# High and low parts of weighted expert rows stacked on the two halves of the partitions

## The chip, the cores and the metric

The kernel runs on one core of a Trainium2 chip. The metric is the device time of one launch in microseconds (us). All matrices of the kernel are float32; TensorE (PE) takes them either as float32 or as fp32r, the 32-bit format in which one product takes one pass over the columns.

## The reference

One decoder block over 512 tokens of width 1024. After two attention branches, whose code the change does not touch, a router picks 4 of 32 experts for each token, and the result is

```
gate    = softmax(top-4 logits)
gu      = xb @ w_gate_up[e] + b_gate_up[e]        # xb: rows of the tokens that chose expert e
a       = (clip(u) + 1) * (min(g) * sigmoid(1.702 * min(g)))
yb      = a @ w_down[e] + b_down[e]
y       = segment_sum(yb * gate, token of the row)
out     = x + y
```

## The kernel before

The first 450 us or so are norm, projections, attention and routing. Then comes the expert stage, which the change touches. It works through items. An item is one expert's list of up to 96 tokens (even items, three groups of 32 rows) or up to 64 tokens (odd items, two groups). There are 32 items here: item 0, then a hardware loop (`Fori`) of 15 pairs, each with an odd item (i = 1) and an even item (i = 2), and a last odd item outside the loop.

For each item PE runs `gate_up(i)` (line 1712: 8 slices k of 128 input features, products of 32 stationary columns and 512 moving ones, four side by side on the array) and `down(i)` (line 1751, and line 1759 for the third group). In one turn of the loop PE's order is gate_up(1), the small list products (line 1658), down(0), gate_up(2), lists, down(1). The weights are float32, 2 MB for each DMA: four for gate_up (`gu_head` three, `gu_tail` one) and two for down (`dn_even` or `dn_odd`), issued by SP in a fixed order. Each has one buffer, and SP issues the next transfer into it when PE has read it (`gu_used`, `bank_done`, `dn_used`).

`down` leaves the rows of an item in PSUM: bank 5 holds slots 0 to 63 on partitions 0 to 63 with columns 0 to 511 of the model width, and the same slots on partitions 64 to 127 with columns 512 to 1023. Bank 4 holds the third group of an even item, in the same two halves. They are weighted by the tokens' gates and split in two fp32r tiles: ScalarE (ACT) writes the high part `y_hi` (`weigh`, line 849), and when all of an item's are written (`y_high`) VectorE (DVE) writes the rest `y_lo` (`keep_low`, line 1245) and signals `y_kept`. An even item has two such tiles (n = 0, 1), an odd one has one (n = 2).

The sum over experts for each token is made on PE by one-hot tables: `put_odd`, `put_even` and `put_even_b`, made by POOL, have a 1 where slot (partition) belongs to token (column); partitions 64 to 127 repeat the slots of 0 to 63. For each 128 tokens (a chunk c, of four) `sums` (line 1678) multiplies the chunk's columns of a table with `y_hi` and `y_lo`. Partitions 0 to 63 go into the bank of columns 0 to 511 and partitions 64 to 127 into the bank of 512 to 1023. `add_sums` on DVE (line 1253) adds both banks to the residual `x_tok`.

The order around it is written out by hand. The four chunks of a pair of items (the even item of this turn's down(0) and the odd item of the turn before) stand inside gate_up(2), after the slices k = 1, 3, 5 and 6 (`SUM_STEPS`). Chunk 0 waits for `y_kept` of the pair (line 1686). The semaphore `gu_used` of slice k = 1 is raised ahead of that wait. After the loop, `gate_up(1, last=True)` holds down(0) after k = 3, chunk 0 after k = 5 and chunk 1 after k = 6; chunks 2 and 3, down(1) and the four last sums (the last item alone, one table) follow, and SP stores each chunk of `x_tok` as it is complete. In all there are 64 full chunks and 4 last ones. On DVE, `keep_low(i - 1)` is the last step of a turn's half, behind `activate(i)`; on ACT, `weigh(i - 1)` stands behind `sigmoid(i)`.

Of the kernel before, what the change touches and what calls it, by code (L numbers as in the profile page):

```python
# [20 lines left out]
F32 = mybir.dt.float32  # L21
F32R = mybir.dt.float32r
BF16 = mybir.dt.bfloat16
I32 = mybir.dt.int32
ALU = mybir.AluOpType
ACT = mybir.ActivationFunctionType
AX = mybir.AxisListType

P = 128
HD = 64  # L30
# [26 lines left out]
def hybrid_block(nc, x, positions, norm1_g, w_in, b_forget, b_gate, q_norm_swa, k_norm_swa, sinks,  # L57
                 q_norm_fox, k_norm_fox, w_o_swa, w_o_fox, w_out, norm2_g, w_router, b_router,
                 w_gate_up, b_gate_up, w_down, b_down, out):
    T, D = x.shape[1:]  # L60
# [38 lines left out]
    with ExitStack() as ctx:  # L99
# [30 lines left out]
        xreg, r1, r2, work, const = Region(16 * K), Region(32 * K), Region(36 * K), Region(10 * K), Region(17 * K)  # L130
# [50 lines left out]
        xT = r2.put("xT", [P, KD, SLOTS])  # L181
        aT = r2.put("aT", [P, KD, SLOTS])
        y_at = r2.at
        y_hi = [r2.put(f"y_hi{n}", [P, D // 2], F32R) for n in range(3)]
        y_lo = [r2.put(f"y_lo{n}", [P, D // 2], F32R) for n in range(3)]
        y_end = r2.at
        sel = r2.put("sel", [P, NB, 2, P], BF16)

# [83 lines left out]
        put_odd = in_place_of("w_rt", "put_odd", [P, T], F32R)  # L272
# [52 lines left out]
        gate_all = r1.put("gate_all", [P, ITEMS, 2])  # L325

        ps = ctx.enter_context(nc.psum_tensor("ps", [P, 8, 512], F32))
# [75 lines left out]
        y_high, y_kept, put_ready = sem("y_high"), sem("y_kept"), sem("put_ready")  # L403
# [155 lines left out]
        def _(pool):  # L559
            steps = [0]  # L560

            def then(ins):

                steps[0] += 1
                ins.then_inc(pool_step, 1)
                pool.wait_ge(pool_step, steps[0])

            g = nc.gpsimd
# [43 lines left out]
            for i in range(E):  # L612
                ins = g.memset(place_rank[:, i:i + 1], float(E - 1 if i == 0 else i // 2 if i % 2 else N_SMALL + i // 2 - 1))
# [37 lines left out]
            pool.wait_ge(items_ready, 1)  # L651
            n_pairs = pool.value_load(pairs[0:1, 0:1], min_val=PAIRS, max_val=MAX_PAIRS)
            pool.wait_ge(bdn_ps, 8)
            g.memset(y_hi[2][:, :].bitcast(F32), 0.0)
            then(g.memset(y_lo[2][:, :].bitcast(F32), 0.0))
            g.tensor_copy(put_odd[:, :], y_lo[2][:, :].bitcast(F32)).then_inc(put_ready, 1)
            then(g.tensor_copy(put_row[:, 1:3], row_all[:, 0, :]))
            put(put_even, 1)
            put(put_even_b, 2)
# [24 lines left out]
        def _(act):  # L684
            sc = nc.scalar
# [24 lines left out]
            for k in range(KD):  # L710
                act.wait_ge(hT_ps, k + 1)
                sc.activation(hT_h[:, k, :], ps[:, k % 4, :], ACT.Identity,
                              scale=vcol[:, k:k + 1]).then_inc(hT_hi, 1)
# [18 lines left out]
            for g in range(G_GATE, G_O):  # L732
                c = g - G_GATE
                split_high(g + 1)
                if g == G_O - 1:
# [3 lines left out]
                    for r in (0, 64):  # L739
                        ins = sc.activation(c_rows[r:r + 32, :], ps[r:r + 32, 7, :], ACT.Copy, scale=-1.0 / SCALE)  # L740
# [17 lines left out]
                for d in (0, 1):  # L758
                    j = 2 * c + d
                    ins = sc.activation(gates_T[:, j, :], ps[:, g % 2 * 2 + d, :], ACT.Sigmoid,  # L760
                                        bias=vcol[:, 16 + j:17 + j])
# [4 lines left out]
            for n in range(1, len(QKT), 2):  # L766
                s, j = QKT[n]
                act.wait_ge(qkT_ps, n + 1)
                dst, src, scale = turned(s, j)
# [10 lines left out]
            for n in range(NU):  # L780
# [3 lines left out]
                if n >= 4:  # L784
# [3 lines left out]
                              scale=SCALE, accum_out=den[:, n:n + 1]).then_inc(probs, 1)  # L788
# [24 lines left out]
            for m in range(N_OUT):  # L813
# [5 lines left out]
                for c in range(NB):  # L819
                    s = slice(m * GW, (m + 1) * GW)  # L820
                    ins = sc.activation(h2n[:, c, s], x_tok[:, c, s], ACT.Square, accum_out=ssq_g[:, m, c:c + 1])
# [22 lines left out]
            def weigh(i, pair=None):  # L844

                col = slice(i, i + 1) if pair is None else bass.ds(pair * 2 + i, 1)
                act.wait_ge(dn_used[1], counted(2, i + 1, pair))
                for a in (0,) if i % 2 else (0, 1):
                    ins = sc.activation(y_hi[i % 2 * 2 + a][:, :], ps[:, 5 - a, :], ACT.Identity,
                                        scale=gate_all[:, col, a:a + 1].rearrange("p a n -> p (a n)"))  # L850
                ins.then_inc(y_high, 1)

            sigmoid(0)
# [12 lines left out]
        def _(dve):  # L866
            v = nc.vector
# [24 lines left out]
            for k in range(KD):  # L892
                dve.wait_ge(hT_hi, k + 1)
                v.scalar_tensor_tensor(out=hT_l[:, k, :], in0=ps[:, k % 4, :], scalar=vcol[:, k:k + 1],
                                       in1=hT_h[:, k, :].bitcast(F32), op0=ALU.mult,
                                       op1=ALU.subtract).then_inc(hT_ready, 1)
# [11 lines left out]
            for n in range(3):  # L908
                ins = v.tensor_scalar(above[:, n:n + 1], row, float(GROUP * (n + 1)), None, ALU.is_ge)
# [4 lines left out]
                                        op0=ALU.mult, op1=ALU.add))  # L914
            then(v.tensor_scalar(place_of[:, 1:2], place_of[:, 1:2], float(SMALL), None, ALU.add))
            then(v.scalar_tensor_tensor(out=place_of[:, 0:1], in0=above[:, 1:2], scalar=-2.0 * GROUP, in1=row,
                                        op0=ALU.mult, op1=ALU.add))
# [12 lines left out]
            for part in (C1, C2, C3):  # L930
                then(v.scalar_tensor_tensor(out=ang[:, :, :], in0=ang_k[:, :, :], scalar=-part, in1=ang[:, :, :],
                                            op0=ALU.mult, op1=ALU.add))
            v.tensor_scalar(ang[:, :, :], ang[:, :, :], 3.1415925, -3.1415925, ALU.min, ALU.max).then_inc(ang_ready, 1)
            v.tensor_scalar(sink_neg[:, :], sink_bc[:, :], -1.0, None, ALU.mult)
            for g in range(2, G_GATE + 1):
                split_low(g)
                if g == G_GATE:
# [8 lines left out]
                                   op0=ALU.mult, op1=ALU.max).then_inc(fl_abs, 1)  # L946
# [4 lines left out]
            for g in range(G_GATE, G_O):  # L951
                c = g - G_GATE
# [7 lines left out]
                if c == 1:  # L960
# [5 lines left out]
                    for a in (0, 1):  # L966
# [5 lines left out]
                                                    in1=g2, op0=ALU.mult, op1=ALU.mult))  # L972
                if 2 <= c < NB + 2:
# [4 lines left out]
                    for a, h0, h1 in ((0, 0, HQ), (1, HQ, SWA_H)):  # L978
                        n = h1 - h0
# [6 lines left out]
                    for half in (0, 1):  # L986
                        ins = v.tensor_tensor(k_dup[:, c, :, half, :], rot[:, 0, HQ:SWA_H, :], rot[:, 1, HQ:SWA_H, :],
                                              ALU.add)
                    ins.then_inc(qk_ready, 1)
                if g == G_GATE + 5:  # L990

                    dve.wait_ge(fl_ln, 1)
                    for at in range(0, P, 32):
                        ins = v.scalar_tensor_tensor(out=lf[:, :, at:at + HF], in0=fl[:, :, :], scalar=0.0,
                                                     in1=fl_a[:, :, :], op0=ALU.min, op1=ALU.subtract)
# [3 lines left out]
            for r in (32, 96):  # L999
                ins = v.scalar_tensor_tensor(out=c_rows[r:r + 32, :], in0=ps[r:r + 32, 7, :], scalar=-1.0 / SCALE,  # L1000
                                             in1=c_hi[r:r + 32, :].bitcast(F32), op0=ALU.mult, op1=ALU.subtract)
            ins.then_inc(c_ready, 1)

            for n in range(0, len(QKT), 2):
                s, j = QKT[n]
                dve.wait_ge(qkT_ps, n + 1)
                dst, src, scale = turned(s, j)
# [16 lines left out]
            for p in range(NP + 3):  # L1024
                if p < NP:
                    n = 2 * p
                    c, b, h = units[n]
# [4 lines left out]
                    if b == 0:  # L1032
                        v.scalar_tensor_tensor(out=nb[:, two], in0=mx[:, two], scalar=-SCALE, in1=sink_neg[:, h:h + 2],
                                               op0=ALU.mult, op1=ALU.min).then_inc(shift, 1)
# [77 lines left out]
            for c in range(NB):  # L1112
                ins = v.scalar_tensor_tensor(out=lg[:, c, :], in0=ps[:, 7, c * E:(c + 1) * E], scalar=rstd[:, 1, c:c + 1],
                                             in1=brt[:, :], op0=ALU.mult, op1=ALU.add)
# [124 lines left out]
            def keep_low(i, pair=None):  # L1239

                col = slice(i, i + 1) if pair is None else bass.ds(pair * 2 + i, 1)
                dve.wait_ge(y_high, counted(2, i + 1, pair))
                for a in (0,) if i % 2 else (0, 1):
                    n = i % 2 * 2 + a
                    ins = v.scalar_tensor_tensor(out=y_lo[n][:, :], in0=ps[:, 5 - a, :],
                                                 scalar=gate_all[:, col, a:a + 1].rearrange("p a n -> p (a n)"),
                                                 in1=y_hi[n][:, :].bitcast(F32), op0=ALU.mult, op1=ALU.subtract)
                ins.then_inc(y_kept, 1)

            def add_sums(c, n, banks=SUM_BANKS):  # L1250
# [121 lines left out]
        def _(pe):  # L1372
# [298 lines left out]
            def sums(parts, c, n, banks=SUM_BANKS):  # L1671

                pe.wait_ge(sums_added, n)
                for at, (table, y) in enumerate(parts):
                    for half in (y_hi[y], y_lo[y]):
                        for h in (0, 1):
                            rows = slice(h * HD, (h + 1) * HD)
                            ins = pe.matmul(ps[:, banks, :][:, h], table[rows, c * P:(c + 1) * P], half[rows, :],  # L1678
                                            start=(at == 0 and half is y_hi[y]),
                                            stop=(at == len(parts) - 1 and half is y_lo[y]))  # L1680
                return ins

            def pair_sums(c, pair, banks=SUM_BANKS, added=None):
# [140 lines left out]
```

## Time and profile before

| | |
|---|---|
| median of 3 runs | 1443.29 us (1440.86 to 1443.79) |
| the profiled execution: its span, from first to last instruction | 1443.0 us |
| PE busy | 1375.7 us (95%) |
| DVE busy | 747.1 us (52%) |
| ACT busy | 220.7 us (15%) |
| moved by DMA | 447.27 MB, mean 310 GB/s |
| granted TensorE clock, mean | 0.989 |

For the profiled execution the page gives no time beside its span; the median of the runs lies 0.29 us above that span. Busy times overlap, so they do not add up to the span. A row of the timeline gives the start of a group of instructions, the time from the start of its first to the end of its last, and their number.

### The profile page before, as it was taken

The numbers are of one execution on the slowest core, as the hardware profiler recorded it, in microseconds if no ns is written. First come the engines' busy times: TensorE is split into PE (matmuls) and PEld (weight loads), VectorE is DVE, ScalarE is ACT, GpSimd is POOL, SyncE is SP. The second block draws the span as 40 slices with busy tenths as digits, with TensorE's granted clock in tenths as the row PEclk, the third lists the DMA queues.
The fourth block names the chain that finished last, engine by engine and source line by source line (L and its number), as shares of the span: only waits on it lengthen the run. The fifth ranks groups of instructions, "written<-read, shape, count | busy, mean of one in ns | idle before, by whom it ended". The sixth has DMA issues, their size and how long they took to land.

```text
span 1443.0 us, 27407 instructions
## 1 busy us (share of the span) xinstructions
PE 1375.7 (95%) x11224; PEld 660.7 (46%) x11227; DVE 747.1 (52%) x1472; ACT 220.7 (15%) x398; POOL 185.6 (13%) x234
## 2 busy tenths in 40 slices
PE   6999999999988999999999999999999999999997
PEld 5888887878952333333232323323232332323233
DVE  5213745666256565645556444555654455565444
ACT  4224435552220000000000000000000000000000
POOL 2001400000002021120211202021120202112020
PEclk9999999999999999999999999999999999999999
DMA  6232320002769999999999999999999999999992
GB/s 190 88 117 67 109 88 1 2 30 89 277 242 354 414 386 413 399 410 413 412 413 400 419 395 413 411 413 414 400 421 401 413 411 412 411 399 419 401 412 119
DMA packets 59127, 447.27 MB, mean 310 GB/s; under 512 B 8592, under 2 KB 26032, under 8 KB 34480
## 3 DMA queue, kind: packets, MB, share of 16 engines
q1 hardware_dynamic: 55904, 435.96, 75.5%
q0 software_dynamic: 3072, 10.49, 2.3%
q8 instruction: 27, 0.44, 0.1%
q10 hardware_dynamic: 112, 0.28, 0.1%
q14 instruction: 12, 0.10, 0.0%
HBM read 442.51 MB, written 4.19 MB: 310 GB/s over the span
## 4 chain that ended last, share of the span: by engine, by line
PE 76%; DMA 20%; DVE 2%; ACT 1%; issue 1%; SPq 0%; DVEq 0%; ACTq 0%
PE ps L1712 31%; DMA gu_head<-in_w_gate_up_dram 11%; PE ps L1751 10%; DMA gu_tail<-in_w_gate_up_dram 8%; PE ps L1678 6%; PE ps L1406 3%; PE ps L1408 3%; PE ps L1407 3%; PE ps L1759 2%; PE ps L1543 2%; PE ps L1432 2%; PE ps L1431 2%; PE ps L1430 2%; PE ps L1397 1%; PE ps L1398 1%; PE ps L1399 1%
## 5 line engine op out<-in xcount | busy, mean ns | idle before, releaser
L1712 PE MATMUL ps<-gu_head,xT 128*32 128x512 f32 x3840 | 428.0, 596 | 8.2 <-DVE xT L1209 4.9
L1712 PEld LDWEIGHTS ps<-gu_head,xT 128*32 128x32 f32 x3840 | 120.5, 110 | 292.0 <-issue 276.0
L1253 DVE TENSOR_TENSOR x_tok<-x_tok,ps 128x1024 f32<-128x1024 f32 x68 | 82.7, 1220 | 255.8 <-PE ps L1678 255.8
L1712 PE MATMUL ps<-gu_tail,xT 128*32 128x512 f32 x1280 | 157.3, 630 | 27.7 <-DMA gu_tail<-in_w_gate_up_dram 27.7
L842 ACT ACTIVATE act_s<-act_gu 128x768 f32<-128x768 f32 (+1 forms) x32 | 23.6, 738 | 935.6 <-DVE act_gu L1228 935.6
L1205 DVE STREAM_TRANSPOSE xT<-xg 32x256 f32<-32x256 f32 x308 | 132.9, 432 | 3.8
L1217 DVE STREAM_TRANSPOSE act_gu<-ps 128x512 f32<-128x512 f32 x80 | 57.2, 715 | 143.3 <-PE ps L1712 138.2
L638 POOL DMA_INDIRECT xg<-h_dram,idx_g x32 | 70.0, 2187 | 446.1 <-DVE row_all L1187 446.1
L1751 PE MATMUL ps<-dn_even,aT 128*32 128x512 f32 x1024 | 116.1, 594 | 0.0
L879 DVE TENSOR_TENSOR st_l<-st_w,st_h 128x2048 fp32r<-128x2048 f32 x25 | 57.3, 2292 | 113.2 <-ACT st_h L702 113.2
L1751 PE MATMUL ps<-dn_odd,aT 128*32 128x512 f32 x1024 | 113.2, 594 | 2.2 <-DVE aT L1236 2.2
L1712 PEld LDWEIGHTS ps<-gu_tail,xT 128*32 128x32 f32 x1280 | 38.6, 114 | 128.5 <-issue 89.9
L1751 PEld LDWEIGHTS ps<-dn_odd,aT 128*32 128x32 f32 x1024 | 31.6, 110 | 70.0 <-issue 67.0
L1751 PEld LDWEIGHTS ps<-dn_even,aT 128*32 128x32 f32 x1024 | 31.7, 110 | 68.0 <-issue 67.6
L1759 PE MATMUL ps<-dn_even,aT 128*32 128x512 f32 x512 | 60.8, 592 | 0.0
L702 ACT CAST st_h<-st_w 128x2048 fp32r<-128x2048 f32 x25 | 47.7, 1908 | 32.7 <-PE ps L1432 30.1
L666 POOL COPY put_row<-row_all 128x1 f32 x15 | 2.8, 186 | 383.9 <-PE ps L1678 383.9
L1406 PE MATMUL ps<-hT_h,st_h 128*128 128x512 f32 x128 | 50.0, 391 | 0.0
L1430 PE MATMUL ps<-st_h,hT_h 128*128 128x512 f32 x128 | 49.9, 390 | 0.0
L1408 PE MATMUL ps<-hT_h,st_l 128*128 128x512 f32 x128 | 49.8, 389 | 0.0
L1407 PE MATMUL ps<-hT_l,st_h 128*128 128x512 f32 x128 | 49.8, 389 | 0.0
L1432 PE MATMUL ps<-st_h,hT_l 128*128 128x512 f32 x128 | 49.8, 389 | 0.0
(361 smaller groups left out, 1814.4 us busy)
## 6 DMA issues: line engine op xcount, KB each, us to landing
gu_head<-in_w_gate_up_dram SPq DMA_DIRECT2D x96, 2048.0 KB
gu_tail<-in_w_gate_up_dram SPq DMA_DIRECT2D x32, 2048.0 KB, 20.3
dn_even<-in_w_down_dram SPq DMA_DIRECT2D x32, 2048.0 KB, 25.1
dn_odd<-in_w_down_dram SPq DMA_DIRECT2D x32, 2048.0 KB, 21.3
st_w<-in_w_in_dram SPq DMA_DIRECT2D x17, 1024.0 KB, 5.2
st_w<-in_w_out_dram SPq DMA_DIRECT2D x4, 1024.0 KB, 5.4
x_tok<-in_x_dram SPq DMA_DIRECT2D x4, 512.0 KB, 6.0
st_w<-in_w_o_swa_dram SPq DMA_DIRECT2D x4, 512.0 KB, 3.5
```

The costliest lines, as they stand in the source:

```text
L638: g.indirect_dma_start(out=xg[0:n, :], out_offset=None, in_=h2_dram[:, :], in_offset=bass.IndirectOffsetOnAxis(ap=idx_g[0:n, 0:1], axis=0) ...
L1205: ins = v.transpose(xT[r, :, s].rearrange("r (k a) s -> r k a s", a=2), near[s, r].rearrange("s p k a -> s k a p"))
L1253: v.tensor_tensor(x_tok[:, c, :].rearrange("p (h n) -> p h n", h=2), x_tok[:, c, :].rearrange("p (h n) -> p h n", h=2), ps[:, banks, :], A ...
L1406: pe.matmul(dst, wh[:, k], xh[:, k], start=(k == 0), stop=False)
L1407: pe.matmul(dst, wh[:, k], xl[:, k], start=False, stop=False)
L1408: ins = pe.matmul(dst, wl[:, k], xh[:, k], start=False, stop=(k == n - 1))
L1430: pe.matmul(dst, hT_h[:, k0 + k, rows], st_h_wide[half][:, k], start=(half == 0 and k == 0), stop=False)
L1432: ins = pe.matmul(dst, hT_l[:, k0 + k, rows], st_h_wide[half][:, k], start=False, stop=(half == 1 and k == KH - 1))
L1678: ins = pe.matmul(ps[:, banks, :][:, h], table[rows, c * P:(c + 1) * P], half[rows, :], start=(at == 0 and half is y_hi[y]), stop=(at == l ...
L1712: ins = pe.matmul(ps[j * GROUP:(j + 1) * GROUP, n, :], xT[:, k, n * GROUP:(n + 1) * GROUP], gu_columns(k, j), start=(k == 0), stop=(k == K ...
L1751: ins = pe.matmul(ps[u * GROUP:(u + 1) * GROUP, 5, :], aT[:, 4 * j + k, u % 2 * GROUP:(u % 2 + 1) * GROUP], dn_chunk(i, j)[:, k * D + u // ...
L1759: ins = pe.matmul(ps[u * GROUP:(u + 1) * GROUP, 4, :], aT[:, 4 * j + ku, 2 * GROUP:], dn_chunk(i, j)[:, ku * D + u // 2 * 512:ku * D + (u ...
```

## The change

Instead of a tile of high parts and one of low parts, each tile now holds one half of the model width (h = 0: columns 0 to 511, h = 1: columns 512 to 1023), with the high parts on the partitions that have this half in PSUM and the low parts on the other 64 partitions. ACT writes 64 partitions at a time, and DVE reads PSUM and the high part on one half of the partitions and writes on the other half. `sums` then contracts all 128 partitions in one product for each table and half of the width. The tiles take the same place. The lines that zero `y_half[2]` at the start are renamed only.

```diff
-        y_hi = [r2.put(f"y_hi{n}", [P, D // 2], F32R) for n in range(3)]
-        y_lo = [r2.put(f"y_lo{n}", [P, D // 2], F32R) for n in range(3)]
+        y_half = [[r2.put(f"y_half{n}{h}", [P, D // 2], F32R) for h in (0, 1)] for n in range(3)]
...
                 for a in (0,) if i % 2 else (0, 1):
-                    ins = sc.activation(y_hi[i % 2 * 2 + a][:, :], ps[:, 5 - a, :], ACT.Identity,
-                                        scale=gate_all[:, col, a:a + 1].rearrange("p a n -> p (a n)"))
+                    for h in (0, 1):
+                        high = slice(h * HD, (h + 1) * HD)
+                        ins = sc.activation(y_half[i % 2 * 2 + a][h][high, :], ps[high, 5 - a, :], ACT.Identity,
+                                            scale=gate_all[high, col, a:a + 1].rearrange("p a n -> p (a n)"))
                 ins.then_inc(y_high, 1)
...
                 for a in (0,) if i % 2 else (0, 1):
-                    n = i % 2 * 2 + a
-                    ins = v.scalar_tensor_tensor(out=y_lo[n][:, :], in0=ps[:, 5 - a, :],
-                                                 scalar=gate_all[:, col, a:a + 1].rearrange("p a n -> p (a n)"),
-                                                 in1=y_hi[n][:, :].bitcast(F32), op0=ALU.mult, op1=ALU.subtract)
+                    for h in (0, 1):
+                        high, low = slice(h * HD, (h + 1) * HD), slice((1 - h) * HD, (2 - h) * HD)
+                        y = y_half[i % 2 * 2 + a][h]
+                        ins = v.scalar_tensor_tensor(out=y[low, :], in0=ps[high, 5 - a, :],
+                                                     scalar=gate_all[high, col, a:a + 1].rearrange("p a n -> p (a n)"),
+                                                     in1=y[high, :].bitcast(F32), op0=ALU.mult, op1=ALU.subtract)
                 ins.then_inc(y_kept, 1)
...
                 for at, (table, y) in enumerate(parts):
-                    for half in (y_hi[y], y_lo[y]):
-                        for h in (0, 1):
-                            rows = slice(h * HD, (h + 1) * HD)
-                            ins = pe.matmul(ps[:, banks, :][:, h], table[rows, c * P:(c + 1) * P], half[rows, :],
-                                            start=(at == 0 and half is y_hi[y]),
-                                            stop=(at == len(parts) - 1 and half is y_lo[y]))
+                    for h in (0, 1):
+                        ins = pe.matmul(ps[:, banks, :][:, h], table[:, c * P:(c + 1) * P], y_half[y][h][:, :],
+                                        start=(at == 0), stop=(at == len(parts) - 1))
```

## Rows read from the trace of the kernel before

**Rows 1.** The page's slices of 36 us: DMA share in tenths, and GB/s.
```profile
DMA  6232320002769999999999999999999999999992
GB/s 190 88 117 67 109 88 1 2 30 89 277 242 354 414 386 413 399 410 413 412 413 400 419 395 413 411 413 414 400 421 401 413 411 412 411 399 419 401 412 119
```
**Rows 2.** Busy time by stretch: us, busy of each engine, clock, DMA share, GB/s.
```profile
510.00:515.00 5.00, 5.00 (x56) 1.59 (x52) 4.73 (x11) 0.00 (x0) 3.71 (x3) 1.00 0.72 239
...
860.00:920.00 60.00, 57.47 (x528) 18.20 (x520) 33.31 (x67) 3.32 (x5) 9.49 (x7) 1.00 1.01 411
```
**Rows 3.** PE's waits on weights, timeline: start, us, instructions, [idle before, releaser].
```profile
900.29 3.64 PE L1712 MATMUL ps<-gu_tail,xT 128*32 128x512 f32 x32 [2.10 <-DMA gu_tail<-in_w_gate_up_dram]
...
914.98 5.36 PE L1712 MATMUL ps<-gu_head,xT 128*32 128x512 f32 x48 [0.43 <-DMA gu_head<-in_w_gate_up_dram]
...
1341.48 5.34 PE L1712 MATMUL ps<-gu_tail,xT 128*32 128x512 f32 x32 [2.92 <-DMA gu_tail<-in_w_gate_up_dram]
```
**Rows 4.** The chain of waits, around one chunk of sums and the list products.
```profile
842.44 0.19 PE ps L1658 x4
...
865.10 1.59 PE ps L1678 x12
```
**Rows 5.** PE's timeline, a run of products of 128 rows by 512 columns, first and last.
```profile
59.71 0.39 PE L1431 MATMUL ps<-st_l,hT_h 128*128 128x512 f32 x1
...
65.15 0.39 PE L1431 MATMUL ps<-st_l,hT_h 128*128 128x512 f32 x1
```
**Rows 6.** PE's timeline, inside one chunk of sums.
```profile
920.27 0.50 PE L1678 MATMUL ps<-y_hi,put_odd 64*128 64x512 f32 x2
920.61 0.39 PE L1678 MATMUL ps<-y_lo,put_odd 64*128 64x512 f32 x2
...
921.53 0.40 PE L1678 MATMUL ps<-y_lo,put_even_b 64*128 64x512 f32 x2
```
**Rows 7.** Groups of ACT and DVE: busy us, mean ns | idle before; then single lines.
```profile
L849 ACT ACTIVATE y_hi<-ps,gate_all 128x512 fp32r<-128x512 f32 x48 | 31.0, 680 | 25.6 <-PE ps L1759 14.6 <-PE ps L1751 9.1
...
L1245 DVE SCALAR_TENSOR_TENSOR y_lo<-ps,gate_all,y_hi 128x512 fp32r<-128x512 f32 x48 | 34.5, 746 | 21.1 <-ACT y_hi L849 19.8
...
L740 ACT ACTIVATE c_rows<-ps x2: 572/582/592, 205.3 to 205.9; 32x512 fp32r<-32x512 f32 x2
...
207.31 1.39 DVE L1000 SCALAR_TENSOR_TENSOR c_rows<-ps,c_hi 32x512 fp32r<-32x512 f32 x2
```
**Rows 8.** Timeline of the last turn of the loop: ACT, DVE and PE.
```profile
1357.61 1.26 ACT L849 ACTIVATE y_hi<-ps,gate_all 128x512 fp32r<-128x512 f32 x2
...
1359.03 1.41 DVE L1245 SCALAR_TENSOR_TENSOR y_lo<-ps,gate_all,y_hi 128x512 fp32r<-128x512 f32 x2
...
1362.53 0.50 PE L1678 MATMUL ps<-y_hi,put_odd 64*128 64x512 f32 x2
```
**Rows 9.** Timeline after the loop, down to the final sums.
```profile
1409.59 1.26 ACT L849 ACTIVATE y_hi<-ps,gate_all 128x512 fp32r<-128x512 f32 x2 [14.57 <-PE ps L1759]
...
1411.00 1.41 DVE L1245 SCALAR_TENSOR_TENSOR y_lo<-ps,gate_all,y_hi 128x512 fp32r<-128x512 f32 x2 [13.90 <-ACT y_hi L849]
...
1412.79 0.50 PE L1678 MATMUL ps<-y_hi,put_odd 64*128 64x512 f32 x2
...
1424.92 7.07 PE L1751 MATMUL ps<-dn_odd,aT 128*32 128x512 f32 x64 [2.18 <-DVE aT L1236]
...
1433.00 0.75 DVE L1245 SCALAR_TENSOR_TENSOR y_lo<-ps,gate_all,y_hi 128x512 fp32r<-128x512 f32 x1 [5.87 <-ACT y_hi L849]
1433.97 0.50 PE L1678 MATMUL ps<-y_hi,put_odd 64*128 64x512 f32 x2 [1.97 <-DVE y_lo L1245]
...
1434.60 0.64 PE L1678 MATMUL ps<-y_hi,put_odd 64*128 64x512 f32 x2
1434.85 4.61 DVE L1253 TENSOR_TENSOR x_tok<-x_tok,ps 128x1024 f32<-128x1024 f32 x4 [1.10 <-PE ps L1678]
1435.02 0.64 PE L1678 MATMUL ps<-y_lo,put_odd 64*128 64x512 f32 x2
```

More of the change, by code:

```diff
@@ L653, in _ @@
             pool.wait_ge(bdn_ps, 8)
-            g.memset(y_hi[2][:, :].bitcast(F32), 0.0)
-            then(g.memset(y_lo[2][:, :].bitcast(F32), 0.0))
-            g.tensor_copy(put_odd[:, :], y_lo[2][:, :].bitcast(F32)).then_inc(put_ready, 1)
+            g.memset(y_half[2][0][:, :].bitcast(F32), 0.0)
+            then(g.memset(y_half[2][1][:, :].bitcast(F32), 0.0))
+            g.tensor_copy(put_odd[:, :], y_half[2][1][:, :].bitcast(F32)).then_inc(put_ready, 1)
             then(g.tensor_copy(put_row[:, 1:3], row_all[:, 0, :]))
```

## The prediction

> **What bounds the kernel now.** I read the page's 40 slices first. From slice 14 on, where the expert stage runs, DMA is at nine tenths or more and moves about 410 GB/s [rows 1], while PE is also nearly always busy, so the two have to be told apart. The stretches do that: 860 to 920 us has a DMA share of 1.01 with PE busy 57.5 of 60 us [rows 2]. The timeline of PE then shows where PE's 2 to 3 idle us go: it waits for weights, 2.10 us at 900, 0.43 at 915, 2.92 at 1341 [rows 3], a pattern that repeats from 648 us on (20 waits, small ones included). So in the middle of the loop the bound is the stream of weights, and PE has a little slack in each turn, about 2.5 to 3 us in 60.
>
> At both ends it is otherwise. The last wait of PE on weights is at 1341.48 [rows 3]. From there PE runs without a break up to 1422.7, and then the chain goes over DVE and ACT, with waits of 2.18 and 1.97 us [rows 9]. What delays PE after 1341 delays the end. At the start, DMA's share falls to 0.72 at 510 to 515 us [rows 2]: the transfers in flight had run out, and the next one waits for the end of gate_up(2) on PE. What delays PE before that moment delays the stream, which then bounds all that follows.
>
> **The products.** A full chunk has 12 products of 64 rows now. They start two by two, the two halves of the rows at once: the second pair at 920.61 and the sixth at 921.53, that is 0.92 us for four steps, 0.23 us a step, and 0.34 us for the first [rows 6]. A product of 128 rows by 512 columns takes (65.15 - 59.71) / 24 = 0.227 us in a dense run [rows 5], 24 products apart. So six pairs become six full products of the same length. The chunk costs PE 1.59 us now [rows 4], of which 6 x 0.227 = 1.36 is the products and 0.23 the change from the 32-column tiles of gate_up and back. Afterwards the latter is at least 0 and at most what it is now, or 0.1 more if a load of the whole array has to wait for all four tiles. The nearest row is the group of four list products, full-array as well: 0.19 us with that change in it [rows 4]. Five columns a product cost little, so about 0.16 for the change. I take a chunk as 1.52, 0.07 less than now; bounds -0.23 and +0.1. Half as many products, and next to nothing gained, since the halves already ran side by side.
>
> Of the 64 full chunks only those on a PE-bound piece count: four before 511 us, four in the last turn, two after the loop, ten in all. That gives -0.7 us (bounds -2.3 and +1.0). The other 54 lie beside the DMA stream.
>
> **ACT and DVE.** Instructions double: 48 to 96 on each. The length goes by the columns, not the partitions, by the nearest rows: 32x512 out of PSUM takes ACT 0.58 us against 0.68 for 128x512 with a scale, and the two DVE operations on 32 partitions take 1.39 together, against 1.41 for two of 128 [rows 7, 8]. On ACT two in a row take 1.26, a pitch of 0.58; four take 3 x 0.58 + 0.68 = 2.42 or a bit over, 2.45, so +1.19 for an even item and +0.59 for an odd one.
>
> On DVE two in a row take 1.41 with 0.746 each [rows 7, 8], so they overlap by 0.08. The two of line 1000, which lie on partitions 32 and 96, take 1.39 at 0.69 each: no overlap [rows 7]. The new ones alternate between the halves of the partitions, as those do. So four take 4 x 0.75 = 3.0 (bounds: 2.75 with the overlap; 3.2 if crossing the halves costs a further 0.05 each), +1.6 for an even item, and two take 1.5, +0.75 for an odd one. The page "VectorE: DVE Perf Modes" of the Trainium skill, section "Two Vector instructions with no wait between them", has a rule for this: an instruction that starts in another quadrant of partitions than the one before is held until all earlier ones have finished. By that rule it is 3.0, without it 2.75; the trace, with 1.39 against 1.41, agrees with it. Below zero these costs can't go, as nothing is taken off either engine.
>
> ACT is 15% busy and DVE 52%, so their throughput is not the matter. What counts is the chain: down's end, ACT, DVE, sums of chunk 0. Queued behind keep_low on DVE are the next list choice (1.6 us, needed some 20 us later) and add_sums of chunk 0, which moves back by less than the 5 us until PE asks for it. Behind weigh on ACT there is nothing for over 20 us.
>
> **The waits that this makes.** In a turn like the last one, y_hi starts at 1357.61 and PE starts chunk 0 at 1362.53 [rows 8]. After: ACT ends at 1357.61 + 2.45 = 1360.06; DVE starts 0.16 later as now, and ends at 1363.2; PE follows 0.22 later (from 1433.75 to 1433.97 now [rows 9]), at 1363.4: a new wait of **0.9 us**. In turns where PE has first waited for gu_head, as at 914.98, chunk 0 comes some 0.6 us later against ACT, and the wait is about 0.3. In the middle of the loop both are paid out of PE's idle time on weights: the queue of transfers is 20 us deep, and the buffer of slice 1 is handed back ahead of the wait. At two places they are not hidden:
> - the first turn, before the dry spell of DMA at 510: +0.9 (bound below 0, if the stream makes it up);
> - the last turn, after 1341: +0.9 (bound below 0.6, with DVE's overlap).
>
> **After the loop** down(0) ends only two slices of gate_up ahead of chunk 0. y_hi starts at 1409.59, y_lo ends at 1412.41 and PE starts at 1412.79 [rows 9]: 0.16 us of slack. After: 1409.59 + 2.45 + 0.16 + 3.0 + 0.22 = 1415.4, a new wait of **2.6 us** (2.3 with DVE's overlap) in PE's path. Behind it are the rest of gate_up(1), its turning by DVE and down(1), so it is paid in full.
>
> **At the very end** weigh(1) and keep_low(1) lie bare between down(1) and the last sums: 0.59 + 0.75 = **+1.34 us**. The last sums have two steps a chunk before and after, and DVE's four additions at 1.15 us each bound them [rows 9], so only the first chunk counts. PE's wait grows from 1.97 to 3.3 us. A wait of 2.92 was followed by the half clock (32 products in 5.34 us), 2.10 and 2.18 by the full one (32 in 3.64) [rows 3, 9]. So I take half clock for the first chunk: 0.42 and 0.64 (the rows at 1434.60 and 1435.02 [rows 9]), 1.1 us instead of 0.88: +0.25.
>
> **The clock after the new wait of 2.6.** A wait of 2.9 us costs 5.34 - 3.64, 1.7 us, by the lower clock of 1.2 GHz; one of 2.1 costs nothing [rows 3]. 2.55 lies midway between 2.18 and 2.92, so I can't name a nearer row, and take half the price, +0.85 (bounds 0 and 1.7).
>
> **The sum**, against the profiled execution: first turn 0.9, last turn 0.9, after the loop 2.6, end 1.34 + 0.25, clock 0.85, products -0.7. That is 6.1 us on 1443.0; the median is 0.3 above that span, and I keep that distance: 1443.3 + 6.1 = **1449.4**. With the terms at their small ends (0, 0.6, 2.3, 1.3, 0, -2.3 for the products) it is +1.9, 1445.2; with the large ones (0.9, 1.1, 2.8, 1.7, 1.7, +1.0) it is +9.2, 1452.5.
>
> **Rivals.**
> *The waits are paid in every turn.* If the DMA stream follows PE more closely than its share of 1.01 says, 14 more turns pay, half of them 0.9 and half 0.3, 8.4 us: 1457.8. For it: each weight tile has one buffer, so transfers start when PE lets go. Against it: in the middle of the loop PE waits for DMA and not the reverse [rows 2, 3]. 10%.
> *The new waits stay hidden*, since half the partitions are done in less time than the 32-partition rows say, and only the bare end is paid: 1.34 + 0.25 - 0.7 = +0.9, 1444.2. Both operations would have to take about half of now. Rows 7 speak against it. 10%.
> *The other side: a chunk of full products takes half of its time.* The halves then only seem to run side by side and the 12 products really cost 12 issues. A chunk would fall from 1.59 to 0.8; ten exposed ones give -8 against +6.8 of the other terms: 1442.1, not slower. It decides from 0.68 us saved a chunk on, and would be plain in PE's busy time. Against it: the dense step of 0.227 us [rows 5] can't be beaten by the same instruction. If the dry spell of DMA at 510 is spared as well, it comes to 1440. 5%.
> *The clock gives back.* If the later arrival shortens the wait at 1341 below about 2.2 us, 1.7 us return. Its turn has a new wait of only 0.3, less four chunks at -0.07, so the wait stays 2.9. 5%: 1447.7, within the range.
>
> **Numbers.** The forecast's case has 70%, with a range of its own of 1445.2 to 1452.5. A difference of 0.2%, 2.9 us, is about what a measurement can tell. Slower by over that holds for nearly all of the forecast's case, the clock's rival and the first rival: 0.79. Within it: the hidden case, most of the third rival, and the low end of the forecast: 0.17. Faster: 0.04. The range of 8 in 10 reaches down to the hidden case and leaves the rival at 1458 out: 1444.0 to 1453.5.
>
> **What would show it.** Right: 96 operations on each of lines 849 and 1245 at unchanged length; even items with a row of four of 2.45 us on ACT and 3.0 on DVE; chunks of six products at 1.4 to 1.6 us; a wait of PE on DVE before chunk 0, some 0.9 or 0.3 us in the loop and 2.6 after it; DMA share still 1.01 in the loop, and PE's waits on weights shorter by what the new ones take. Wrong: chunks clearly under 1.4 us; operations on 64 partitions shorter than 0.5 us; turns longer than 63 us in the middle of the loop.

## The result, and the profile after

| | before | after |
|---|---|---|
| median (lowest to highest) | 1442.47 us (1440.86 to 1443.79), 4 runs | 1451.88 us (1449.37 to 1453.5), 4 runs |
| ratio, 95% interval | | 1.006 (1.0038 to 1.0081) |
| span of the profiled execution | 1443.0 us | 1451.7 us (its run took 1453.5) |

The change makes the kernel 0.6% slower: 9.4 us between the medians, 8.7 between the profiled spans. The forecast was 1449.4, with 1444.0 to 1453.5 as range. A run's time lies about 1.8 us above its own span (1453.5 and 1451.7 here), so the profiled execution of before belongs to a run of about 1444.8 (an estimate from this distance). Both profiled executions are thus on the slow side of their kernels, by about the same amount.

The page of the changed kernel, part 5 (busy us, mean ns | idle before) and part 2 (DMA's busy tenths in slices, nine or more through the loop as before). The instructions of ACT and DVE are twice as many, at the length of before:

```profile
L1248 DVE SCALAR_TENSOR_TENSOR y_half<-ps,gate_all,y_half 64x512 fp32r<-64x512 f32 x96 | 72.0, 750 | 48.1 <-ACT y_half L850 46.7
...
L850 ACT ACTIVATE y_half<-ps,gate_all 64x512 fp32r<-64x512 f32 x96 | 65.6, 683 | 27.7 <-PE ps L1759 13.7
...
DMA  6232320003678999999999999999999999999981
```

DVE had 746 ns and ACT 680 at 128 partitions [rows 7]: 64 partitions cost as much as 128.

The chain of waits after, one chunk of sums in the last turn of the loop. It is six products of 128 rows in 1.59 us, where it was twelve of 64 rows in 1.59 [rows 4]:

```profile
1364.81 5.29 PE ps L1712 x48
1370.09 1.59 PE ps L1679 x6
```

PE's timeline after, with what it idled for ([idle before, releaser]): two turns in the middle of the loop, and then from the last wait on weights to the end. Against [rows 3, 8, 9]:

```profile
963.54 5.19 PE L1712 MATMUL ps<-gu_tail,xT 128*32 128x512 f32 x32 [2.41 <-DMA gu_tail<-in_w_gate_up_dram]
985.73 0.71 PE L1679 MATMUL ps<-y_half,put_odd 128*128 128x512 f32 x2 [1.23 <-DVE y_half L1248]
1026.25 3.64 PE L1712 MATMUL ps<-gu_tail,xT 128*32 128x512 f32 x32 [0.51 <-DMA gu_tail<-in_w_gate_up_dram]
1040.83 5.36 PE L1712 MATMUL ps<-gu_head,xT 128*32 128x512 f32 x48 [0.31 <-DMA gu_head<-in_w_gate_up_dram]
1046.89 0.71 PE L1679 MATMUL ps<-y_half,put_odd 128*128 128x512 f32 x2 [0.70 <-DVE y_half L1248]
1088.95 5.34 PE L1712 MATMUL ps<-gu_tail,xT 128*32 128x512 f32 x32 [2.04 <-DMA gu_tail<-in_w_gate_up_dram]
...
1340.84 5.34 PE L1712 MATMUL ps<-gu_tail,xT 128*32 128x512 f32 x32 [2.54 <-DMA gu_tail<-in_w_gate_up_dram]
1363.17 0.71 PE L1679 MATMUL ps<-y_half,put_odd 128*128 128x512 f32 x2 [1.22 <-DVE y_half L1248]
...
1416.42 0.70 PE L1679 MATMUL ps<-y_half,put_odd 128*128 128x512 f32 x2 [2.94 <-DVE y_half L1248]
...
1418.52 2.97 PE L1712 MATMUL ps<-gu_tail,xT 128*32 128x512 f32 x16
...
1430.11 8.77 PE L1751 MATMUL ps<-dn_odd,aT 128*32 128x512 f32 x64 [2.18 <-DVE aT L1237]
1442.31 3.77 PE L1679 MATMUL ps<-y_half,put_odd 128*128 128x512 f32 x8 [3.43 <-DVE y_half L1248]
```

The lines with "DVE y_half" as releaser are the new waits; only the one at the very end takes the place of an old one (1.97 us before [rows 9]). "Half clock" below means a stretch in which PE was granted the lower of its two clocks, 1.2 instead of 2.4 GHz: 32 products of gate_up behind a wait then take up to 5.34 us where they take 3.64 at the full one.

The two kernels have their last wait on weights within 0.7 us of each other (1341.48 and 1340.84), so the loop has lost nothing that one can see here. In these two traces all of the loss lies behind that point: 101.5 us remained before, 110.9 remain now. Piece by piece, from starts in this fence and in [rows 3, 8, 9]:

| piece | before | after | lost |
|---|---|---|---|
| last wait on weights to chunk 0 of the last turn | 21.05 | 22.33 | 1.3 |
| to chunk 0 after the loop | 50.26 | 53.25 | 3.0 |
| to the last down | 12.13 | 13.69 | 1.6 |
| to the last sums | 9.05 | 12.20 | 3.1 |
| to the end | 9.03 | 9.39 | 0.4 |

In the loop the waits on weights have shrunk: 0.51 + 0.31 + 2.04 from 1026 to 1089, where the same two turns had 1.72 + 0.42 + 2.85 before. The 2.1 us that are gone are about what the two new waits take, 1.93. Over the whole loop, the last wait on weights included, the waits on weights fell from 30.7 us (20 of them) to 18.8 (17), against 13.7 us in 14 new waits. Of those on `gu_tail`, five were followed by half clock after and six before, at 1.7 us each. So the agreement at 1341 holds some luck of the clock, and two single traces can't exclude a cost of a microsecond or so in the loop; e3 below has its bounds.

ACT's and DVE's timeline after, behind the last turn of the loop:

```profile
1410.21 2.77 ACT L850 ACTIVATE y_half<-ps,gate_all 64x512 fp32r<-64x512 f32 x4 [13.74 <-PE ps L1759]
1439.05 1.38 ACT L850 ACTIVATE y_half<-ps,gate_all 64x512 fp32r<-64x512 f32 x2 [10.81 <-PE ps L1751]
```
```profile
1413.13 3.04 DVE L1248 SCALAR_TENSOR_TENSOR y_half<-ps,gate_all,y_half 64x512 fp32r<-64x512 f32 x4 [14.53 <-ACT y_half L850]
...
1440.58 1.51 DVE L1248 SCALAR_TENSOR_TENSOR y_half<-ps,gate_all,y_half 64x512 fp32r<-64x512 f32 x2 [8.26 <-ACT y_half L850]
```

### The profile page after: what moved, and what is told of

Read it like the earlier page. It is cut to its first block, busy times and chain, and to the rows that moved or that the text cites. A ratio compares the mean times of both kernels' runs of the same rounds, so it can differ in the third digit from the quotient of the medians.

```text
span 1451.7 us, 26818 instructions
## 1 busy us (share of the span) xinstructions
PE 1377.7 (95%) x10835; PEld 662.1 (46%) x10835; DVE 784.6 (54%) x1520; ACT 256.8 (18%) x446; POOL 185.6 (13%) x234
## 4 chain that ended last, share of the span: by engine, by line
PE 63%; DMA 15%; DVE 12%; issue 4%; ACT 4%; DVEq 2%; ACTq 0%; SPq 0%; POOL 0%
PE ps L1712 26%; DMA gu_tail<-in_w_gate_up_dram 14%; PE ps L1679 7%; DVE xT L1206 6%; PE ps L1409 3%; PE ps L1751 3%; PE ps L1411 3%; PE ps L1410 3%; ACT y_half L850 2%; PE ps L1546 2%; PE ps L1435 2%; PE ps L1434 2%; PE ps L1433 2%; DVE y_half L1248 2%; DVE act_gu L1227 1%
## 5 line engine op out<-in xcount | busy, mean ns | idle before, releaser
L1248 DVE SCALAR_TENSOR_TENSOR y_half<-ps,gate_all,y_half 64x512 fp32r<-64x512 f32 x96 | 72.0, 750 | 48.1 <-ACT y_half L850 46.7
L850 ACT ACTIVATE y_half<-ps,gate_all 64x512 fp32r<-64x512 f32 x96 | 65.6, 683 | 27.7 <-PE ps L1759 13.7
L1679 PE MATMUL ps<-y_half,put_odd 128*128 128x512 f32 x136 | 50.0, 455 | 21.3 <-DVE y_half L1248 21.3
L1679 PEld LDWEIGHTS ps<-y_half,put_odd 128*128 128x128 f32 x136 | 21.6, 196 | 76.5 <-issue 75.0
L701 ACT CAST st_h<-st_w 128x2048 fp32r<-128x2048 f32 x25 | 47.7, 1908 | 32.1 <-PE ps L1435 30.1
```

The costliest lines, as they stand in the source:

```text
L850: ins = sc.activation(y_half[i % 2 * 2 + a][h][high, :], ps[high, 5 - a, :], ACT.Identity, scale=gate_all[high, col, a:a + 1].rearrange("p ...
L1248: ins = v.scalar_tensor_tensor(out=y[low, :], in0=ps[high, 5 - a, :], scalar=gate_all[high, col, a:a + 1].rearrange("p a n -> p (a n)"), i ...
L1679: ins = pe.matmul(ps[:, banks, :][:, h], table[:, c * P:(c + 1) * P], y_half[y][h][:, :], start=(at == 0), stop=(at == len(parts) - 1))
```

## The experiments

The theory: all of the loss is the longer chain down, ACT, DVE, sums, where neither the stream of weights nor other work covers it, and half clock behind the longest of its waits. The rivals: the products, or PE's change from the tiles of 32 columns to the whole array, cost it; or each turn of the loop pays; or the amount of work on ACT and DVE does it, not its place.

| run | what | median us | runs | ratio to before, 95% interval |
|---|---|---|---|---|
| e1_tiles_only | ACT and DVE of after, products of before | 1452.25 | 6 | 1.0062 (1.0043 to 1.0081) |
| e2_products_only | products of after alone | 1440.61 | 12 | 0.9988 (0.9976 to 1.0) |
| e3_loop_only | the change in the loop alone | 1445.25 | 12 | 1.0006 (0.9993 to 1.0019) |
| e4_tail_only | the change after the loop alone | 1449.42 | 10 | 1.0042 (1.0028 to 1.0055) |
| e5_signal_each | a signal for each ACT instruction | 1444.67 | 12 | 1.0015 (1.0004 to 1.0026) |
| e7_kept_busy | idle products in PE's last waits | 1447.92 | 11 | 1.0038 (1.0026 to 1.0049) |
| e8_signal_each_busy | both | 1443.59 | 12 | 1.0006 (0.9997 to 1.0015) |

The kernel before had 1442.94 (27 runs) beside the first four and 1442.86 (28 runs) beside the others; e6 below was run once, 1450.4. The changed kernel itself was not run again beside them, so it is compared by the ratios.

**e1: the tiles alone.**
```diff
-                    for h in (0, 1):
-                        ins = pe.matmul(ps[:, banks, :][:, h], table[:, c * P:(c + 1) * P], y_half[y][h][:, :], ...)
+                    for part in (0, 1):
+                        for h in (0, 1):
+                            rows = slice(h * HD, (h + 1) * HD)
+                            ins = pe.matmul(ps[:, banks, :][:, h], table[rows, c * P:(c + 1) * P], y_half[y][part][rows, :], ...)
```


> ACT and DVE as in the changed kernel (half-partition instructions, high and low parts stacked), but the sums go back to the 12 products of 64 rows with the operands' shapes of before, each half of the rows into its own bank (so the two halves of the width are not put together as they should be). Theory (the doubled instructions of ACT and DVE lengthen the chain down -> ACT -> DVE -> sums, and that is the whole loss): the time of the changed kernel, 1450 to 1453 us, a chunk of sums 1.6 us, a wait of 2.9 us before chunk 0 after the loop. Rival (the full-array products, or the change of array mode into them, cost the time): back to 1442 to 1444. My theory would fall below 1448.

In this kernel the low parts go to the wrong half of the width, which leaves its time comparable but not its result. Measured 1452.25, with the changed kernel's ratio (1.0062, against 1.006). Its trace has the same three waits and the same slow last down, with the twelve products back:

```profile
1414.16 1.00 PE L1681 MATMUL ps<-y_half,put_odd 64*128 64x512 f32 x4 [2.93 <-DVE y_half L1248]
1427.83 8.77 PE L1753 MATMUL ps<-dn_odd,aT 128*32 128x512 f32 x64 [2.18 <-DVE aT L1237]
1440.03 2.13 PE L1681 MATMUL ps<-y_half,put_odd 64*128 64x512 f32 x16 [3.43 <-DVE y_half L1248]
```
So the products are not what costs. The last sums ran at full clock here (all in 2.13 us), where the changed kernel has 3.77.

**e2: the products alone.**
```diff
-                    for half in (y_hi[y], y_lo[y]):
-                        for h in (0, 1):
-                            rows = slice(h * HD, (h + 1) * HD)
-                            ins = pe.matmul(ps[:, banks, :][:, h], table[rows, c * P:(c + 1) * P], half[rows, :], ...)
+                    for h, half in enumerate((y_hi[y], y_lo[y])):
+                        ins = pe.matmul(ps[:, banks, :][:, h], table[:, c * P:(c + 1) * P], half[:, :], ...)
```


> The kernel before with only the products changed: six of 128 rows a chunk over the old tiles (the bank of a half then gets high parts of both halves or low parts of both, not the right sum). Theory: a chunk costs 1.59 us as with twelve, so the time is that of before, 1441 to 1444 us. Rival 1 (full products are cheaper by 0.07 to 0.2 us, as I had it for the ten exposed chunks): 0.7 to 2 us less. Rival 2 (they cost the time): 1450 and more.

This kernel leaves out that high and low parts must be added to the right half of the width; it is of use for its time alone. Measured 1440.61, 0.9988 of before, with an interval that ends at 1.0. That is 0.4 us under the range of my theory and within what I had given for rival 1, cheaper products. The chain of waits of its trace:

```profile
855.37 1.59 PE ps L1676 x6
856.96 5.29 PE ps L1709 x48
```
And its timeline of PE, the last wait on weights and chunk 0 after the loop:
```profile
1336.88 3.64 PE L1709 MATMUL ps<-gu_tail,xT 128*32 128x512 f32 x32 [1.88 <-DMA gu_tail<-in_w_gate_up_dram]
...
1406.96 0.50 PE L1676 MATMUL ps<-y_hi,put_odd 128*128 128x512 f32 x1
```
A chunk costs 1.59 us, as with twelve products, and from chunk 0 after the loop to the end this trace has 30.1 us (1406.96 to 1437.1) where before had 30.2. So the trace gives no support to rival 1: the 1.7 us by which the ratio lies under 1 don't come from the length of a chunk. One difference has just this size: the last wait on weights, 1.88 us here, was followed by full clock (3.64 us for 32 products, 5.34 before). Whether that holds in its other runs, or the 1.7 us are chance, was not tested.

**e3 and e4: the change in the loop alone, and after it alone.** Both carry a switch for the form of each item's tiles and products:
```diff
+            def weigh(i, pair=None, stacked=True):        # e4: False
...
-            weigh(0, n_pairs)
+            weigh(0, n_pairs, False)                      # e4: True; the same for weigh(1), keep_low(0) and keep_low(1)
```


> Stacked tiles and full products in the 15 turns of the loop, the form of before for the two items after it. Theory (in the loop the new waits of 0.6 and 1.2 us lie beside the stream of weights, except in the last turn, where 1.2 us show, and at the first, where the stream runs dry up to 1 us longer): 1443.7 to 1445 us, and waits on weights shorter by what the new ones take. Rival (the loop pays in every turn): 15 waits, 14 us in all, of which most would show, 1450 or more.

> The other half: the form of before in the loop, stacked tiles and full products for the two items after it. Theory: nearly the whole loss is here: a wait of 2.9 us before chunk 0, 1.6 us of half clock behind it, 1.7 us of half clock in the last down, 1.45 us of ACT and DVE at the end, 0.4 in the last sums: 8 us, 1450 to 1451.5. Rival (the loop pays): 1443 to 1445. If clock is not part of it: 1447.

e3 gives 1.0006 (1445.25 us, 0.25 over the range that I gave), e4 1.0042; of the sum of both, seven eighths lie after the loop. The sum is 0.0048 and the whole change has 0.006; what is missing is about the 1.7 us of the last down, which was slow only with the whole change (below). In e3 all 15 turns have the new wait, and nearly nothing of it shows: its last turn

```profile
1341.26 5.34 PE L1730 MATMUL ps<-gu_tail,xT 128*32 128x512 f32 x32 [2.19 <-DMA gu_tail<-in_w_gate_up_dram]
1363.59 0.71 PE L1697 MATMUL ps<-y_half,put_odd 128*128 128x512 f32 x2 [1.22 <-DVE y_half L1258]
```
has the 1.22 us that are exposed (22.33 from one start to the other, 21.05 before). The rival that every turn pays is out: it asked for 1450 or more, and e3's interval ends 2.7 us over before. In e4 the wait of 2.93 and the end of 3.43 are there, but the last down ran at full clock (64 products in 7.07 us), and the time lies 0.6 us under the range that I gave:

```profile
1415.94 1.03 PE L1692 MATMUL ps<-y_half,put_odd 64*128 64x512 f32 x4 [2.93 <-DVE y_half L1258]
1429.58 7.07 PE L1769 MATMUL ps<-dn_odd,aT 128*32 128x512 f32 x64 [1.22 <-DVE aT L1241]
```
Its wait before that down is 1.22 instead of 2.18, in e3 too (1.23). Some 0.6 us of the difference is PE's: in the mixed form a chunk takes 1.80 us instead of 1.59, and chunks 2 and 3 stand there. The other 0.4 is DVE's: the instruction that writes aT took 0.69 us in both, and 1.06 before; why, no run shows. So e3 and e4 differ from halves of the change in these two things, which cancel in e3: from chunk 0 to the last down it has 12.14 us, and before 12.13.

**e5: a signal for each instruction.** The same instructions, the same number, another order of waits:
```diff
-                ins.then_inc(y_high, 1)                            # after the last one only
+                        sc.activation(...).then_inc(y_high, 1)     # after each
...
-                dve.wait_ge(y_high, counted(2, i + 1, pair))
+                        dve.wait_ge(y_high, counted(6, i * 4 + a * 2 + h + 1, pair))   # before each
```


> The changed kernel, but ACT signals after each of its instructions instead of after the last, and each DVE instruction waits for its own only, so that the two engines overlap. As much work on both as in the changed kernel. Theory (the loss is the serial chain at the places where nothing covers it): in the loop DVE starts behind its activation as in the kernel before and is done with four in 3.04 us, no wait of PE before chunk 0; after the loop 0.69 + 0.16 + 3.04 + 0.22 us against 3.2 available, a wait of 0.9 us and no half clock behind it; at the end one DVE instruction more, 0.8 us. Together 2 to 3 us over the kernel before, 1444 to 1446. Rival (it is the amount of work on ACT and DVE, or their traffic, not its order): 1450 and more.

Measured 1.0015, 1444.67 us, as expected. There is no wait before chunk 0 in any turn of the loop, and 0.86 after it:

```profile
1409.98 0.71 PE L1678 MATMUL ps<-y_half,put_odd 128*128 128x512 f32 x2 [0.86 <-DVE y_half L1247]
1422.08 7.07 PE L1750 MATMUL ps<-dn_odd,aT 128*32 128x512 f32 x64 [2.17 <-DVE aT L1236]
1431.88 2.13 PE L1678 MATMUL ps<-y_half,put_odd 128*128 128x512 f32 x8 [2.73 <-DVE y_half L1247]
```
With all of the added work in place, three quarters of the loss are gone (by the ratios 2.2 us are left of 8.7). It was the work's place in the chain, not its amount.

**e6: two instructions on the same half in a row.**
```diff
-                for a in (0,) if i % 2 else (0, 1):
-                    for h in (0, 1):
+                for h in (0, 1):
+                    for a in (0,) if i % 2 else (0, 1):
```


> The changed kernel with the loops over the half and over the tile exchanged, so that two instructions on the same partitions follow each other before the halves change. If the lost overlap comes from a change of partitions between two instructions (theory), a group of four takes 2.77 - 0.11 x 2 = 2.55 us on ACT and 3.04 - 2 x 0.08 = 2.88 on DVE. If it comes from having 64 partitions instead of 128 (rival), 2.77 and 3.04 stay.

ACT and DVE, timeline after the loop:
```profile
1407.56 2.53 ACT L850 ACTIVATE y_half<-ps,gate_all 64x512 fp32r<-64x512 f32 x4 [13.73 <-PE ps L1759]
1435.93 1.38 ACT L850 ACTIVATE y_half<-ps,gate_all 64x512 fp32r<-64x512 f32 x2 [10.81 <-PE ps L1751]
```
```profile
1410.23 2.85 DVE L1248 SCALAR_TENSOR_TENSOR y_half<-ps,gate_all,y_half 64x512 fp32r<-64x512 f32 x4 [14.28 <-ACT y_half L850]
```
2.53 and 2.85, against 2.77 and 3.04. The overlap of two instructions (0.12 on ACT, 0.09 on DVE) comes back for the pairs on the same partitions, and the odd item, whose two instructions still change halves, stays at 1.38. So it is the change of partitions that costs the overlap, on both engines. A change of the PSUM bank (tile a) doesn't explain it: of the three steps in the changed kernel's group of four the middle one changes the bank too, and none overlaps.

**e7 and e8: PE kept busy while it waits.**
```diff
+            def keep_busy(bank, n):
+                for _ in range(n):
+                    pe.matmul(ps[:, bank, :], ones_b[:, :], bc(ones_b[:, :], 1, 4), start=True, stop=True)
...
+                    keep_busy(6, warm)      # chunk 0 after the loop; 11, in e8 2
                     pe.wait_ge(y_kept, pair * 2 + 2)
...
+            keep_busy(4, 7)
             down(1, n_pairs)
+            keep_busy(4, 12)                # in e8 10
             pe.wait_ge(y_kept, n_pairs * 2 + 3)
```


> The changed kernel with idle products on PE (128x512, results overwritten) in its three waits after the loop: 11 before chunk 0, 7 before the last down, 12 before the last sums, each group shorter than the wait. Theory (part of the loss is the TensorE clock, which falls after a wait of nearly 3 us): the first chunk takes 1.6 instead of 2.2 us, the 16 products behind it 1.9 instead of 2.9, the last down 7.1 instead of 8.8 us, the last sums 0.4 less: 1448 to 1449 us. The waits themselves stay 2.9 and 3.4 us between useful products. Rival (the clock is not part of it): 1451 to 1453.

> Both: a signal for each ACT instruction, and idle products (2, 7 and 10) in the waits after the loop. Theory: as with the signals alone, less the half clock of the last sums, 0.4 us: 1443.5 to 1445.5. If it came out below the kernel before (under 1441), the products of 128 rows would have been worth something after all.

e7: 1447.92. That is 0.1 us under the expected range. The pieces behind the waits are back at full speed, while the chain over ACT and DVE is as long as before (2.77 and 3.04 us):

```profile
1413.99 0.71 PE L1679 MATMUL ps<-y_half,put_odd 128*128 128x512 f32 x2 [0.46 <-DVE y_half L1248]
...
1415.56 1.92 PE L1718 MATMUL ps<-gu_tail,xT 128*32 128x512 f32 x16
...
1426.09 7.07 PE L1757 MATMUL ps<-dn_odd,aT 128*32 128x512 f32 x64 [0.66 <-DVE aT L1237]
1436.59 2.13 PE L1679 MATMUL ps<-y_half,put_odd 128*128 128x512 f32 x8 [0.73 <-DVE y_half L1248]
```
That is 2.97 to 1.92, 8.77 to 7.07 and 3.77 to 2.13 for the three pieces. Of the last only 0.5 us reaches the end (from the start of the last sums 8.9 us, and 9.4 in the changed kernel), since DVE's four additions bound it. Together with chunk 0 (1.57 us for 2.10) the pieces give 3.7 us; the medians differ by 4.0, and the ratios by 3.2. So 3 to 4 us of the loss were clock. e8 gives 1.0006, with 1 inside its interval: with signals for each instruction and PE kept busy the stacked form costs what the old one does. It doesn't beat it, and no run pointed to a version that would.

## Why the prediction was right, and where its sizes were off

**What bounds the kernel** held: the middle of the loop is bound by the stream of weights, the end by the chain. e3 and e4 show it directly.

**The number** was right with some luck. The change cost 9.4 us for a forecast of 6.1, and that is more than the 9.2 to which the forecast's own terms add up at their large ends. The time lies under that end, 1452.5, only because the forecast's base of 1443.3 is 0.8 above the median of before. The +0.9 for the first turn was not seen and the -0.7 for the products was nothing, and these two nearly cancel. What was too small is the clock, and after it ACT.

**The products** were right in kind and off by their small term. I expected 1.52 us a chunk from the list products; it is 1.59. So the -0.7 us of the sum comes to 0 by the traces. The step of 0.227 us in a dense run [rows 5] was the row that decided, and the cost of going to the full array and back is as large as for two halves.

**DVE** measured 3.04 for 3.0 and 1.51 for 1.5, by the rows of line 1000. That rests on the same rule as in the forecast (the Trainium skill, "VectorE: DVE Perf Modes", section "Two Vector instructions with no wait between them"), and e6 agrees with it: 3.04 with a change of half at each instruction, 2.85 with two in a row.

**ACT** was mis-sized. I took four for 2.45 with the pitch of 0.58 that two instructions on all partitions have. It is 2.77, a pitch of 0.69: no overlap when the partitions change. The row of line 740 [rows 7] had shown it, since the two, on different partitions, start 0.6 us apart (205.3 and 205.9) and take 592 and 572 ns. I used it for the length alone. This is 0.3 us in each new wait of an even item: 1.22 for 0.9 in the loop (0.5 to 0.7 for 0.3 in the turns with a wait on gu_head), 2.94 for 2.6 after it, and 0.1 at the end (1.45 for 1.34).

**The first turn** was counted with 0.9 us. DMA's share at 510 to 515 us did fall further, from 0.72 to 0.52, but the last wait on weights came no later. That wait lies anywhere from 1336.9 to 1342.7 us in the traces of these kernels, and 1.2 us apart in two that differ only after it (before and e4), so an effect of 1 us can't be seen there. e3's 0.9 us by the ratio (-1.0 to 2.7) agree with the last turn's 1.3 alone, and their upper end with both. It stays open. The stretch after, with the columns of [rows 2]:
```profile
510.00:515.00 5.00, 5.00 (x58) 1.47 (x50) 4.77 (x9) 0.00 (x0) 4.66 (x3) 1.00 0.52 154
```

**The clock** was the largest error: 0.85 for what came to 3.3 us, and 0.4 for 0.25 at the end. One half of it was in my bounds: the new wait of 2.94 us was followed by half clock for chunk 0 and the 16 products behind it (1.6 us). The other was in no term: the last down also ran slowly, 8.77 us for 7.07, behind a wait of 2.18 that had cost nothing before. e7 shows that both are clock and that both are gone when PE has work in its waits.

Together: 1.3 (last turn) + 2.9 (wait after the loop) + 3.3 (clock) + 1.45 (the end's chain) + 0.4 (last sums) = 9.35, which is what the table of pieces has (9.4). Of the rivals, the one in which the loop pays is refuted by e3, the one with cheap half-partition instructions by the 683 and 750 ns, and the one with chunks at half the time by e2. In the one where the clock gives back, the wait at 1341 was to stay 2.9; it fell to 2.54, and half clock followed it all the same (in e1, after the same 2.54, it did not).

## What to carry to other kernels

Products of 64 rows on the two halves of the array ran side by side already (a chunk 1.59 us in either form); stacking the operands to fill 128 rows saved instructions and no time. What it cost was on the engines that fill the tiles: an instruction on 64 partitions took as long as one on 128 (683 against 680 ns on ACT, 750 against 746 on DVE), so splitting the work by partitions doubled it, and changing partitions from one to the next also lost their overlap. In a kernel whose middle is bound by transfers, look for the price of a longer chain at the places where the stream has ended; signal each piece rather than the last one, and reckon with half clock behind a wait of 2 us or more (it came behind some waits of 2.01 us up, and behind none shorter, below).

## What the runs showed of the hardware that was not expected

- **The length of one wait does not decide the clock.** Waits on weights of 2.04 (at 1088.95, after) and 2.19 us (at 1341.26, e3) were followed by half clock (32 products in 5.34 us), while 2.54 (e1) and 2.86 (e4) were followed by the full one (3.64). The ten traces together have 113 waits on `gu_tail`, and 48 were followed by half clock. The shortest of these 48 is 2.01 us (at 1215.35, e3), and the longest wait with full clock behind it is 2.98 (at 1085.67, e2):

```profile
1215.35 5.34 PE L1730 MATMUL ps<-gu_tail,xT 128*32 128x512 f32 x32 [2.01 <-DMA gu_tail<-in_w_gate_up_dram]
```
```profile
1085.67 3.64 PE L1709 MATMUL ps<-gu_tail,xT 128*32 128x512 f32 x32 [2.98 <-DMA gu_tail<-in_w_gate_up_dram]
```
  The granted clock of the stretch behind the 2.94 us wait:

```profile
1415.00:1420.00 5.00, 3.58 (x14) 0.73 0.00 0
1430.00:1435.00 5.00, 4.89 (x32) 0.66 0.00 0
1435.00:1440.00 5.00, 3.88 (x40) 1.00 0.00 0
```
  The columns are the length, PE busy, clock (1.00 is the full one, a mean over the stretch), DMA share and GB/s; 1430 to 1435 is the last down. The wait in front of it was 2.17 or 2.18 us in six kernels: half clock where one of 2.5 to 2.9 had come some 12 us earlier (after, e1, e6), full clock where it had not (before, e2, e5). In e4 the early wait of 2.93 was there and the later one was 1.22: full clock. What links the two was not tried.
- **ACT loses its overlap like DVE** when the next instruction lies on other partitions: 0.69 us from one to the next instead of 0.58.
